# Differential attention reworked as a pipeline over heads, with the rotations moved into the projections

## What is computed

```python
q, k, v = _split(h @ w_in, (2048, 2048, 2048))
q = q.reshape(B, T, 16, 2, 64); k = k.reshape(B, T, 16, 2, 64); v = v.reshape(B, T, 16, 128)
q, k = _apply_rope(q, cos, sin), _apply_rope(k, cos, sin)   # x1*cos - x2*sin, x2*cos + x1*sin
lam = exp(sum(lp[0] * lp[1])) - exp(sum(lp[2] * lp[3])) + lambda_init
s = einsum('bqhcd,bkhcd->bhcqk', q, k) * 64 ** -0.5
p = softmax(s, axis=-1)
p = p[:, :, 0] - lam * p[:, :, 1]
o = einsum('bhqk,bkhv->bqhv', p, v)
o = _rms_norm(o, subln_g) * (1.0 - lambda_init)             # over the 128 values of a head
y = o.reshape(B, T, 2048) @ w_out
```

## Time and profile before

| | us |
|---|---|
| median of three runs | 3113.94 (3107.73 to 3114.65) |
| the profiled execution | 3110.49 |
| its span, first to last instruction | 3108.4 |
| TensorE busy | 2724.0 (88%) |
| VectorE busy | 1998.8 (64%) |
| ScalarE busy | 1161.1 (37%) |
| GpSimd busy | 221.9 (7%) |

### The profile page before, as it was taken

The page is one execution under the profiler, slowest core; times in us unless marked ns, Lnnn a source line. Parts: engine busy times, 40 slices in busy tenths (PEclk is TensorE's granted clock), DMA queues, the critical chain, the costliest instruction groups (busy, mean ns, idle before and its releaser), DMA issues.

```text
span 3108.4 us, 45017 instructions
## 1 busy us (share of the span) xinstructions
PE 2724.0 (88%) x18304; PEld 2265.7 (73%) x18304; DVE 1998.8 (64%) x1996; ACT 1161.1 (37%) x1294; POOL 221.9 (7%) x277
## 2 busy tenths in 40 slices
PE   1599979996477999999999879996689999999995
PEld 1488859995266788888888668874567888888884
DVE  7786536763756777777777776346566555555557
ACT  0233336542333333333333324336433333333332
POOL 0000000100000300000000030218003000000001
PEclk9999989996688999999999989998799999999998
DMA  9798711223454787887888558540254555555552
GB/s 354 271 383 309 273 54 65 79 74 110 147 178 136 258 321 295 315 297 271 299 299 322 214 190 314 176 158 0 96 175 160 191 190 189 189 189 189 189 189 81
DMA packets 256808, 636.17 MB, mean 205 GB/s; under 512 B 10238, under 2 KB 17204, under 8 KB 234292
## 3 DMA queue, kind: packets, MB, share of 16 engines
q1 hardware_dynamic: 250530, 621.77, 56.4%
q10 hardware_dynamic: 6162, 12.72, 1.1%
HBM read 632.35 MB, written 2.10 MB: 204 GB/s over the span
## 4 chain that ended last, share of the span: by engine, by line
PE 68%; issue 16%; DVE 10%; DVEq 2%; ACT 2%; POOL 1%; ACTq 1%; POOLq 0%; DMA 0%; SPq 0%
PE pa L551 9%; PE pa L552 9%; PE pa L553 9%; PE pb L551 5%; PE pb L553 5%; PE pb L552 5%; PE py L551 4%; PE py L553 4%; PE py L552 4%; DVE s_wl L461 2%; PE pt L1970 2%; PE pa L1970 2%; PE pb L1970 2%; PE py L1970 1%; PE pt L510 1%
## 5 line engine op out<-in xcount | busy, mean ns | idle before, releaser
L461 DVE TENSOR_TENSOR s_wl<-s_raw,s_wh 128x2048 fp32r<-128x2048 f32 (+1 forms) x396 | 915.3, 2312 | 709.1 <-ACT s_wh L456 706.9
L456 ACT ACTIVATE s_wh<-s_raw 128x2048 fp32r<-128x2048 f32 (+1 forms) x396 | 757.8, 1915 | 1279.2 <-PE pa L553 614.4
L551 PE MATMUL pa<-s_wh,s_hth 128*128 128x512 f32 (+1 forms) x1760 | 701.4, 399 | 32.5 <-issue 16.0
L552 PE MATMUL pa<-s_wl,s_hth 128*128 128x512 f32 (+1 forms) x1760 | 694.2, 394 | 0.0
L553 PE MATMUL pa<-s_wh,s_htl 128*128 128x512 f32 (+1 forms) x1760 | 693.0, 394 | 0.0
L551 PEld LDWEIGHTS pa<-s_wh,s_hth 128*128 128x128 f32 x1760 | 337.0, 191 | 109.8 <-issue 20.3
L553 PEld LDWEIGHTS pa<-s_wh,s_htl 128*128 128x128 f32 x1760 | 336.2, 191 | 71.1
L552 PEld LDWEIGHTS pa<-s_wl,s_hth 128*128 128x128 f32 x1760 | 336.6, 191 | 67.9
L500 DVE SCALAR_TENSOR_TENSOR s_wide<-s_adaw,s_silu_c,s_wide 128x2048 f32<-128x2048 f32 x150 | 353.8, 2359 | 0.2 <-issue 0.2
L551 PE MATMUL py<-s_wh,s_guh 128*128 128x512 f32 x704 | 276.4, 393 | 15.2 <-DVE s_ysum L913 12.7
L551 PE MATMUL pb<-s_wh,s_hth 128*128 128x512 f32 x704 | 274.5, 390 | 3.1 <-DVE s_wl L461 3.1
(11 more groups left out here) (320 smaller groups left out, 2577.2 us busy)
## 6 DMA issues: line engine op xcount, KB each, us to landing
s_raw<-in_ffn_w_in SPq DMA_DIRECT2D x176, 1024.0 KB, 5.2
s_adaw<-in_ada_w SPq DMA_DIRECT2D x160, 1024.0 KB, 5.4
s_raw<-in_ffn_w_out SPq DMA_DIRECT2D x88, 1024.0 KB, 5.3
s_raw<-in_ab_w_in SPq DMA_DIRECT2D x48, 1024.0 KB, 7.6
s_raw<-in_diff_w_in SPq DMA_DIRECT2D x48, 1024.0 KB, 5.3
s_raw<-in_ada_w SPq DMA_DIRECT2D x32, 1024.0 KB, 7.6
s_raw<-in_ab_w_out SPq DMA_DIRECT2D x16, 1024.0 KB, 5.2
s_raw<-in_diff_w_out SPq DMA_DIRECT2D x16, 1024.0 KB, 5.1
```

Of the source, the lines that this page charges most:

```text
L456: act.activation(wh[:, s % 2, :, 0:width], raw[:, s, :, 0:width], ACT.Copy).then_inc(hi_done, 1)
L461: dve.tensor_tensor(wl[:, s % 2, :, 0:width], raw[:, s, :, 0:width], wh[:, s % 2, :, 0:width].bitcast(F32), ALU.subtract).then_inc(lo_done, 1)
L551: pe.matmul(o, a_hi, w_hi, start=start and k == 0, stop=False)
L552: pe.matmul(o, a_hi, w_lo, start=False, stop=False)
```

## The change

- *Rotation.* It is done in place in `qkv`, in four blocks (first and second half of q, of k), each of twelve operations of 16 x 32 = 512 columns and six drains. A block runs as soon as its 1024 columns have been copied out. Temporaries are in `htmp`.
- *Lambda.* Load, sums and exponential move into the projections.
- *Scores.* They alternate between two pairs of banks, `py` and `pa`. Outputs and their turn use the two halves of a bank of `pb`, one bank for each of two heads.
- *Order.* The loops over the heads are unrolled, and an iteration holds work of several heads: TensorE scores(h+2), turned weights(h), turned q and k(h+3), outputs(h), turned outputs(h-1); ScalarE and VectorE as in the diff.
- *Weights.* The two maps are no longer both scaled: the second is multiplied by lambda times the ratio of the sums and added to the first. The factor 1/sum goes into the squares and the norm factor.
- *Norm and split.* GpSimd works out the norm factor of each head in three small operations, one a power of -0.5. VectorE applies it as it reads the output from PSUM; turn, gain, high and low part follow inside the loop. The copy of outputs to `qkv` and the two table loads go.
- *Output projection.* Its unit s waits for the heads that it reads (`ready=at_done`), and its first two units are split by ScalarE and VectorE inside the last iterations.

```diff
+        def rotate(pool, j, half):
+            for i in range(NT):
+                at = j * D + half * (D // 2)
+                x = qkv[:, i, at:at + D // 2].rearrange("p (n c f) -> p n c f", c=2, f=32)
+                x1, x2 = x[:, :, 0], x[:, :, 1]
...
+                pool.tensor_tensor(t1, x1, wave(C_SIN), ALU.mult)
+                pool.tensor_tensor(t2, x2, wave(C_SIN), ALU.mult)
+                pool.drain()
+                pool.tensor_tensor(x1, x1, wave(C_COS), ALU.mult)
+                pool.tensor_tensor(x2, x2, wave(C_COS), ALU.mult)
+                pool.drain()
+                pool.tensor_tensor(x1, x1, t2, ALU.subtract)
+                pool.tensor_tensor(x2, x2, t1, ALU.add)
+                pool.drain()
+            pool.sem_inc(at_rot, 1)
...
+        def at_scores_bank(h, c):
+            return (py, pa)[h % 2][:, c]
+        def at_out_bank(h):
+            return pb[:, h % 2]
...
+            for j in range(2):
+                for half in range(2):
+                    pool.wait_ge(pa_free, 2 + 2 * (17 + FG + 4 * j + 2 * half + 2))
                     pool.sem_inc(passed, 1)
-                    rotate(pool, m * 2 + slot, slot)
+                    rotate(pool, j, half)
...
+            def norm(h):
+                pool.wait_ge(at_sq, h + 1)
+                pool.tensor_scalar(A_s[:, h % 4, 22:24], A_s[:, h % 4, 20:22], 1.0 / P, EPS, ALU.mult, ALU.add)
+                pool.drain()
+                pool.tensor_tensor(A_s[:, h % 4, 22:24], A_s[:, h % 4, 22:24], half_neg.to_broadcast((P, NT)), ALU.pow)
+                pool.drain()
+                pool.tensor_tensor(A_s[:, h % 4, 18:20], A_s[:, h % 4, 22:24], A_s[:, h % 4, 12:14],
+                                   ALU.mult).then_inc(at_rstd, 1)
+            for h in range(DH):
+                norm(h)
...
+            def squares(h):
+                act.wait_ge(at_o, h + 1)
                 for i in range(NT):
-                    if i:
-                        act.drain()
-                    act.activation(A_sq[:], qkv[:, i, bass.ds(h * P, P)], ACT.Square,
...
+            for h in range(-3, DH + 2):
+                if 0 <= h - 1 < DH:
+                    squares(h - 1)
+                if 0 <= h + 1 < DH:
+                    exps(h + 1)
+                if 0 <= h < DH:
+                    turned_p(h)
+                if h + 3 < DH:
+                    turned_qk(h + 3)
+                if h - 2 > 0 and h % 2:
+                    split_high((h - 3) // 2)
+                if h >= DH:
+                    high(act, C_OUT1, h - DH)
...
+            def weights(h):
+                dve.wait_ge(at_exp, h + 1)
+                dve.reciprocal(A_s[:, h % 4, 12:16], A_s[:, h % 4, 8:12])
+                dve.drain()
+                dve.scalar_tensor_tensor(A_s[:, h % 4, 16:18], A_s[:, h % 4, 14:16], small[:, 74:75], A_s[:, h % 4, 8:10],
+                                         ALU.mult, ALU.mult)
+                dve.drain()
+                for i in range(NT):
+                    ins = dve.scalar_tensor_tensor(A_p[:, h % 2, 0, i], A_p[:, h % 2, 1, i], A_s[:, h % 4, 16 + i:17 + i],
+                                                   A_p[:, h % 2, 0, i], ALU.mult, ALU.add)
+                ins.then_inc(at_p, 1)
+            for h in range(-2, DH + 3):
+                if 0 <= h - 2 < DH:
+                    scaled(h - 2)
+                if h >= 4 and h % 2 == 0:
+                    split_low((h - 4) // 2)
+                if 0 <= h + 2 < DH:
+                    maxima(h + 2)
+                if 0 <= h - 1 < DH:
+                    normed(h - 1)
+                if 0 <= h + 1 < DH:
+                    weights(h + 1)
+                if DH <= h < DH + 2:
+                    low(dve, C_OUT1, h - DH)
...
+            pe.wait_ge(pa_free, 2 + 2 * (17 + FG + 12))
+            for h in range(-3, DH + 2):
+                if 0 <= h + 2 < DH:
+                    scores(h + 2)
+                if 0 <= h < DH:
+                    turn_p(h)
+                if h + 3 < DH:
+                    turn_qk(h + 3)
+                if 0 <= h < DH:
+                    outputs(h)
+                if 0 <= h - 1 < DH:
+                    turn_o(h - 1)
+            out_pe(pe, C_OUT1, 17 + FG + 12, 2, ready=at_done)
```

More of the change, by code:

```diff
@@ L556, in multiply, with project @@
             mm.then_inc(unit_done, 1)
-        def project(pe, c, n, lhs, done, free, bank, width=W, call=None, between=None):
+        def project(pe, c, n, lhs, done, free, bank, width=W, call=None, between=None, ready=None):
             for s in range(4):
@@ L1482, in _ @@
-            turned_qk(0, first=True)
-            turned_qk(1)
-            exps(0, 0, first=True)
-            heads(act, act_head)
-            act.drain().then_inc(at_sq, 1)
-            act.wait_ge(at_var, 1)
-            act.activation(A_ss[:], A_ss[:], ACT.Ln)
-            act.drain()
-            act.activation(A_rs[:], A_ss[:], ACT.Exp, scale=-0.5).then_inc(at_rstd, 1)
-            for m in range(DH // 2):
-                act.wait_ge(at_scaled, m + 1)
-                act.activation(hth[:, 2 * m:2 * m + 2], A_t2[:, m % 2], ACT.Copy).then_inc(at_hi, 1)
@@ L1841, in _ @@
                     part_step(dve, 142 + u, 71 + u // 2, u % 2, u - 2, 9)
-            with dve.Fori(5, 12) as t:
-                for s in range(4):
-                    low(dve, t + C_DIFF, s)
-            part_store(dve, 9)
             dve.wait_ge(lam_in, 16)
@@ L1851, in _ @@
             dve.tensor_reduce(A_lam[0:1, 256:258], lam4[:, :, 0], AX_X, ALU.add).then_inc(lam_prod, 1)
+            with dve.Fori(5, 12) as t:
+                for s in range(4):
+                    low(dve, t + C_DIFF, s)
+            part_store(dve, 9)
             dve.wait_ge(lam_exp, 1)
@@ L1918, in _, with maxima @@
-            lower(DH // 2 - 1)
-            dve.drain()
-            dve.wait_ge(at_done, DH // 2)
-            out_dve(dve, C_OUT1, 17 + FG + 12, 2)
+            def maxima(h):
+                dve.wait_ge(at_scores, h + 1)
+                for c in range(2):
+                    dve.tensor_reduce(A_s[:, h % 4, 2 * c:2 * c + 2],
+                                      at_scores_bank(h, c).rearrange("p (i k) -> p i k", k=SEQ), AX_X, ALU.max)
+                dve.drain()
+                dve.tensor_scalar(A_s[:, h % 4, 4:8], A_s[:, h % 4, 0:4], -0.125, None, ALU.mult).then_inc(at_bias, 1)
@@ L2368, in _ @@
-            scores(0, first=True)
-            turn_qk(1, 1)
-            heads(pe, pe_head)
-            for m in range(DH // 2):
-                pe.wait_ge(at_on, m + 1)
-                if m >= 2:
-                    pe.wait_ge(at_scaled, m - 1)
-                for h in range(2):
-                    for i in range(NT):
-                        mm = pe.transpose(pb[:, m % 2, h * SEQ + i * P:h * SEQ + (i + 1) * P],
-                                          A_on[:, m % 2, i, h * P:(h + 1) * P], ident)
-                mm.then_inc(at_oT, 1)
```

236 lines of the change are left out of this document (84 added, 152 removed).

## The result

The kernel with the change takes 3078.32 us in the median of four runs (3073.74 to 3082.94); the kernel before takes 3114.3, also in the median of four. The ratio is 0.9887, with a 95% interval of 0.9864 to 0.991: 1.1% faster, and clear of no change. The forecast was 3083 (range 3068 to 3101). The profiled execution of the changed kernel took 3080.2; its span is 3078.4, 30.0 less than the span of before.

The account below looks back on a forecast made before the run. The attention was taken to be bound by a chain, with TensorE not full in the heads. From 3110.5, minus 33.8 in the attention and plus 5.3 in the projections, the sum was 3082, stated as 3083; range 3068 to 3101.

Parts of the forecast that it names:

- The zero point: Whole kernel: savings count from the profiled execution of before, 3110.5 us, 3.4 under the median of the three shown runs.
- The start and the fill: Attention start: first turn right after the last copy, 2.2 us earlier; at the low clock, outputs(0) end at 2100.
- 5.06: Heads: us per head for the loop outputs, squares, exponentials, copy, outputs between ScalarE and TensorE; taken for thirteen heads.
- two heads at 7.1 and 2 us for a cold episode: Heads: two at 7.1 us with TensorE at 1.2 GHz, plus 2 us for one more low-clock stretch, within 82 us.
- the rival: Heads: VectorE, strictly in order, is the bound at 5.5 to 6.1 us a head; 3093 in all, chance 0.27.
- GpSimd's norm: Heads: three small GpSimd operations per head, the power taken at 1.0 us; at 3.07 the sum loses 2 us.
- one of the signs by which I would have been wrong: Heads: the prediction is wrong if VectorE's application of the norm waits for GpSimd's power.
- The tail: After the last head: first output matmul 5.6 us after outputs(15), instead of 25.9.
- The warmer first unit: Output projection: the old first unit ran half its time at 1.2 GHz; half of that 2.4 us counted as saved.
- The 1.05 of slack: Projections, first rotation block: 6.4 us of delay, less 1.05 that a unit has in hand, gives a 5.3 us loss.
- from the second block on only the low half is there: Projections, later rotation blocks: low half late by 1.1 us at most against 1.05 in hand, so no loss.
- The rival of slower rotations: Projections: 16x32 broadcast operations take much longer than 512 contiguous columns; at 2.5 us each, 3134 in all; chance 0.12.

Follow-up runs that it names:

- rotations_only: The kernel before with only the rotations moved to four blocks beside the projections and the head loop unrolled; 3111.06 us, ratio 0.9999 to the kernel before.
- act_more: The changed kernel with one more 512-wide ScalarE copy of PSUM per head, ahead of the copy of the turned weights, result unused; 3086.31 us.
- one_bank_pair: The changed kernel with a single pair of score banks, so scores of h+2 wait for the exponentials of h+1; 3122.95 us.
- dve_more: The changed kernel with one more 512-wide VectorE maximum of the scores per head, result unused; 3078.67 us.
- squares_later: The changed kernel with ScalarE's squares of head h-1 after the copy of h, VectorE's norm last, output turns a head later; 3067.58 us, ratio 0.9859.

## Why the prediction was right

*The zero point.* It was the profiled execution of before, and the sum was 3082. In the profiled executions the parts that the change touches gave 39.6 us net (46.5 + 0.6 - 7.5), 11.1 more than the 28.5 of the sum; the untouched stages took 9.6 back. These differ from one execution to the next, in kernels in which they are the same code: in thirteen traces the first lies between 1800.0 and 1809.7, the last between 767.2 and 772.8. A place in the last one shows one cause. TensorE resumes after the same pause, in the kernel before and in the changed one:

```profile
3055.68 0.50 PE L551 MATMUL py<-s_wh,s_guh 128*128 128x512 f32 x1 [2.50 <-DVE s_gul L921]
3056.02 0.40 PE L552 MATMUL py<-s_wl,s_guh 128*128 128x512 f32 x1
```

```profile
3022.16 0.80 PE L541 MATMUL py<-s_wh,s_guh 128*128 128x512 f32 x1 [2.50 <-DVE s_gul L907]
3022.76 0.63 PE L542 MATMUL py<-s_wl,s_guh 128*128 128x512 f32 x1
```

Both waited 2.50 us, but the second has lost its clock (0.72 in the 6 us around it, against 1.00), and its matmuls start 0.43 instead of 0.23 apart until 3025. What decides between the two I did not find out. So the forecast is nearer to the result than its terms deserve, and part of that is luck. Term by term: the fill 4.6 us better than taken, the heads 9.3 better, the tail and the first output unit together 0.7 worse, the projections 2.2 worse. That is 11 us in all, and the untouched stages took 9.6 of them back in the two profiled executions. The medians of the result lie 36.0 apart, between the 28.5 of the sum and the 39.6 of the stages.

*The start and the fill.* The first turn follows the last copy at once, as predicted: it starts 0.65 us after the copy's start, at 2.95 before. This is the lambda's share, as rotations_only shows.

```profile
2095.75 0.60 ACT L807 ACTIVATE s_qkv<-pa 128x512 f32<-128x512 f32 x1 [2.12 <-PE pa L543]
2096.40 0.42 PEld L2319 LDWEIGHTS pt<-s_cst,s_qkv 128*128 128x128 f32 x4 [0.47 <-ACT s_qkv L807]
```

Outputs(0) ends 11.2 after that copy; I had 15.8, since I assumed the low clock of the earlier trace rows. The clock is 1.00 through the fill, and the 4.6 us are the term that I had too long.

*The heads.* The loop was the right one and 5.06 was 0.16 too long (4.90). The term "two heads at 7.1 and 2 us for a cold episode" (6 us over the regular period) all but failed to come: the heads took 72.7 against 82. Only the last head sees a low clock (0.72 from 2172 to 2180, with pauses of 1.87 and 3.09 us ahead of outputs(13) and outputs(14)), and outputs(15) take 0.9 us more for it (2.07 instead of 1.16). And I gave the last head a full period; it takes 3.09.

I did not see in the trace of before why its clock fell, and the runs leave it open. From the third to the thirteenth output product the mean clock was 1.00 in the change, with a longest regular pause of TensorE of 1.43 us, 0.88 in act_more (1.92) and 0.72 in one_bank_pair (2.88). But it was also 0.89 in the kernel before and 0.91 in rotations_only, where no regular pause is over 1.2 us, so the longest pause does not order the kernels. The busy share doesn't either, since a product at the low clock counts for nearly twice the time (2.07 against 1.16): the 20.05 busy us of 30 in one_bank_pair are 101 instructions, the 34.97 of 50 in the change 262. And above, the same pause of 2.50 us cost the clock once and once not.

*VectorE.* I had 4.6 of 5.06 us (91%) and gave the rival a chance of 0.27. It was 39.37 of 50 (79%), and dve_more shows that an operation of 0.68 us more is free. From start to start its steps take 4.1 us a head: maxima with bias 1.44, norm 0.52, weights 1.42, scaling 0.40, half a low half 0.35. The norm, which no row showed, was sized right (0.55); what was too much is above all the 0.3 of waits, which I counted as work.

*GpSimd's norm.* The power takes 0.70 us in all sixteen heads, under the 1.0 that I took, and far from the 3.07 of the earlier trace rows; in the head above L1138 runs while L1870, VectorE's maxima from PSUM, does. The Trainium skill (SBUF — State Buffer, Who interferes with whom) gives this by its rule for VectorE operations with at most one SBUF input, and the trace agrees: 0.70 beside the maxima, and 0.70 in the last head with VectorE idle. In one_bank_pair one power meets a VectorE operation with two SBUF inputs (L1864, 0.68 us) and takes 1.25. The factor is there 1.5 to 1.7 us after the squares and delays nobody in the first thirteen heads. In the last three the norm waits 1.3 to 1.5 us for it, one of the signs by which I would have been wrong; for head 15 that can cost the tail 0.4 us at most (the low half could have started when its high half ended at 2182.52, and starts at 2182.96). In squares_later it sits in the loop.

*The tail.* 5.7 against 5.6. Its rows are the predicted ones, the high half (L446) first and the low half last:

```profile
2180.61 1.91 ACT L446 ACTIVATE s_wh<-s_raw 128x2048 fp32r<-128x2048 f32 x1 [0.15 <-issue]
...
2182.96 2.28 DVE L451 TENSOR_TENSOR s_wl<-s_raw,s_wh 128x2048 fp32r<-128x2048 f32 x1
...
2185.34 0.77 PE L541 MATMUL pa<-s_wh,s_hth 128*128 128x512 f32 x1 [1.55 <-issue]
```

The warmer first unit that I put at 1.2 gave 0.6: its matmuls start at the low clock too, for 3.9 us instead of 5.3.

*The rotations.* An operation takes 1.26 to 1.35 when VectorE leaves it alone, as taken (1.3), and a unit 6.5, as worked out (6.6). The projections still lost 7.5 and not 5.3. Two steps failed. The 1.05 of slack that I took off is not there: from the second to the fourth copy pair the two spacings grew by 2.9 and 3.5, together the 6.4 before that subtraction. And "from the second block on only the low half is there" is wrong: the fourth copy was at 1903.23 in the kernel before, the conditioning lasted until 1910, so the two meet again. After the change the second GpSimd block starts at 1912.95 and finds a conditioning step; the next spacing grew by 1.7 (6.4 and 1.7 are 8.1; the way to the second pair was 1.5 shorter, the later ones together 0.9 longer, for which I have no cause; that makes the 7.5):

```profile
1917.62 3.38 DVE L490 SCALAR_TENSOR_TENSOR s_wide<-s_adaw,s_silu_c,s_wide 128x2048 f32<-128x2048 f32 x1
1920.92 3.38 DVE L451 TENSOR_TENSOR s_wl<-s_raw,s_wh 128x2048 fp32r<-128x2048 f32 x1
```

The rival of slower rotations did not come: a broadcast 16 x 32 operation costs what 512 contiguous columns cost. The rule of the Trainium skill on which it leaned (same page and section), an exclusive lock for the whole instruction, fits all the same: VectorE's starts move from 3.30 to 2.75 apart when GpSimd's operation goes from 1.29 to 0.74 us, the same 0.55. What VectorE loses is 1.1 and 0.55 (from starts 2.2 apart), each 0.19 less than the operation.

## What to carry to other kernels

When a loop over engines is opened, walk round the next loop with rows before you count how busy the engines are: here the loop gave 5.06 for 4.90, while the busiest engine is at 79%. Work moved to GpSimd beside a VectorE that is full of operations with two SBUF inputs costs VectorE nearly the length of each GpSimd operation, so cut those operations until the delay fits the slack, or start them when VectorE has some. And compare stages that end at the same event: totals here move by 10 us with code that nobody touched.

## What the runs showed of the hardware

I had not expected how much of a loop's length comes back through the clock. One pair of banks costs 1.77 us a head in waits (6.67 against 4.90), 25 us in all, but 50 us in the attention, where TensorE's granted clock was 0.72 in the mean; 0.49 us a head in act_more became 10.7 instead of 7, at 0.86. What makes the clock fall in these loops stays open. The other surprise is how evenly GpSimd and VectorE take turns when both are always ready: one operation of each, at 3.30 us for the two, for 30 us on end; with GpSimd's operation at 0.74 us the two take 2.75.
